# A hybrid decoder layer: both feed-forward products computed as 2x2 blocks with seven products each

## Chip, core and metric
One NeuronCore of one Trainium2 chip runs the whole program. The metric is the device time of one execution in microseconds (us). TensorE is called PE in the profile (PEld is its weight load), VectorE DVE, ScalarE ACT, GpSimd POOL, SyncE SP.

## What is computed
One step of a one-layer decoder trunk for two groups of requests: a prompt of 1024 tokens and 8 sampled sequences of 4 tokens. The kernel keeps them side by side as T = 1056 columns; activations lie transposed, channels on the 128 partitions. Two gated branches (windowed attention and a gated delta rule), then attention over a memory, then the part that is changed:

```
h = h + xo @ w_xo
u, gv = split(rmsnorm(h, norm_ffn_g) @ w_up, 2)        # w_up 1024 x 5632
u = causal_dwconv(u, ffn_conv_w)                       # 3 taps along the tokens
h = h + (silu(u) * gv) @ w_down                        # w_down 2816 x 1024
y = rmsnorm(h, final_norm_g)
```

With 128-wide tiles, w_up is 8 k tiles by 22 + 22 output tiles (FT = 22), and w_down is 22 k tiles by 8 output tiles.

## The kernel before
**Precision.** Each fp32 operand is split in two fp32r tiles, a head (the rounded value) and a rest (the value minus the head). A product is head x head + head x rest + rest x head, so each k tile of an output tile costs three matmuls for every chunk of columns. T is cut into NCH = 3 chunks of CW = 352 columns.

**Weights.** SP loads a slot of 128 x 1024 into RAW; GpSimd makes WH (head, L767/L768) and WL (rest, L771/L772) from it in pieces 256 wide (`split_pieces`; slots of the first stages in one instruction 1024 wide, L757/L759). Two slots alternate. A slot is free when PE has used it (`w_used`).

**Into the feed-forward.** `xo` is a product of 4 slots; each gives two output tiles, t = 0 to 7. VectorE adds each to H (L2565, `xo_free`), ScalarE makes its head times the gain (XH, L519) and its square (L456), VectorE the rest (XL, L524) and the sum of the squares (L464/L467). The first up product needs XH and XL of all eight. The norm's factor is applied after the product, so that the norm's sum (PE L480, ScalarE L488) is not in front of it.

**The loop.** A step f of 11 handles two tiles of u and two of gv. PE: four `gemm_tile` of 72 matmuls (L544), with PSUM banks 0 to 2 and 3 to 5 in turn, then `down(f-1)`: 8 output tiles, two k tiles each, 18 matmuls a tile (L1987). VectorE: per u tile the factor (L2591), the convolution over 1024 + 32 columns (L2598 to L2605), the product with gv out of PSUM (L2628), the rest of the activation (L2635); per output tile of `down` one addition of PSUM to H, 1056 wide (L2615, `fd_free`). ScalarE: three small copies of the convolution's edge, silu (L1279), the head of the activation (L1285). The last two k tiles of the down projection are computed by column chunks in `end_down` (L2019), each unit added to H (L2654), squared, summed and scaled for the final norm.

**Order.** Each engine runs its own list; semaphores alone bind them, and an engine that waits holds all that is behind it in its list.

## Time and profile before
| | |
|---|---|
| timed runs | 1998.45, 2003.45, 2004.74 us (median 2003.45) |
| profiled execution, first to last instruction | 2002.1 us |
| own time of the profiled execution outside that span | not listed; the median is 1.35 us above the span |
| busy: PE, PEld | 1891.3 us (94%), 1781.6 us (89%) |
| busy: VectorE, ScalarE, GpSimd | 958.1 us (48%), 489.9 us (24%), 832.1 us (42%) |
| feed-forward, from the last xo tile to the last down part | 1211.7 to 1961.3 us |

A busy share says how long an engine had an instruction in it. Matmuls overlap, so one is recorded for about twice the time between two starts; how fast PE goes is read from the distance of starts. In a group's row stand the count, the busy time and the mean ns of one, and behind the second bar the idle time of the engine just before them with what ended it. A wait is shown in square brackets in the timeline.

### The profile page before, as it was taken

How to read it: one execution, taken by the hardware profiler on the slowest of the kernel's cores; microseconds unless marked ns; L12 is line 12 of the kernel's file. 1: busy time of each engine (PE TensorE's matmuls, PEld its weight loads, DVE VectorE, ACT ScalarE, POOL GpSimd, SP SyncE). 2: the span in 40 equal slices, each digit the busy share in tenths (PEclk: the TensorE clock that was granted, in tenths of full speed). 3: DMA queues.
4: the chain of work that ended last, by engine and by line, in shares of the span. 5: the costliest groups of instructions: out<-in, count | busy, mean ns of one | idle time of the engine just before them, and what ended most of it. 6: DMA issues, size and time to landing. Idle time of an engine off the chain costs nothing.

```text
span 2002.1 us, 32389 instructions
## 1 busy us (share of the span) xinstructions
PE 1891.3 (94%) x13273; PEld 1781.6 (89%) x13273; DVE 958.1 (48%) x1150; ACT 489.9 (24%) x908; POOL 832.1 (42%) x907
## 2 busy tenths in 40 slices
PE   6988999999999899999998899999999999999997
PEld 5966799988878788998988599999999999999996
DVE  6877267754454132554142437443453444345346
ACT  6056326643232103421132423100100010000012
POOL 3411033421211233745753025654654565465455
PEclk9999999999999999999999999999999999999999
DMA  4311111110102131422223101111111111111112
GB/s 186 91 38 44 35 43 42 32 65 23 37 27 69 31 107 34 148 96 96 74 76 146 63 26 43 43 42 52 42 42 47 47 42 42 52 42 42 52 46 87
DMA packets 45483, 119.72 MB, mean 60 GB/s; under 512 B 3808, under 2 KB 20896, under 8 KB 44224
## 3 DMA queue, kind: packets, MB, share of 16 engines
q1 hardware_dynamic: 45392, 118.39, 17.7%
q8 instruction: 71, 1.16, 0.2%
q14 instruction: 20, 0.16, 0.0%
HBM read 102.94 MB, written 15.77 MB: 59 GB/s over the span
## 4 chain that ended last, share of the span: by engine, by line
PE 68%; DVE 7%; ACT 3%; issue 1%; POOL 0%; DVEq 0%; ACTq 0%; POOLq 0%
PE PS L544 42%; PE PS L1987 12%; PE PS L1378 3%; PE PS L1576 2%; PE PS L1870 1%; PE PS L1614 1%; PE PS L1770 1%; DVE XL L524 1%; ACT TMP L1223 1%; PE PS L1934 1%; DVE H L2650 1%; PE PS L1955 1%; PE PS L2019 1%; PE PS L1661 0%; PE PS L1927 0%
## 5 line engine op out<-in xcount | busy, mean ns | idle before, releaser
L767 POOL TENSOR_TENSOR WH<-RAW,CST 128x256 fp32r<-128x256 f32 x288 | 195.1, 705 | 827.4 <-PE PS L544 407.0
L544 PE MATMUL PS<-XH,WH 128*128 128x352 f32 x2280 | 505.3, 330 | 33.7 <-POOL WL L759 13.2
L544 PE MATMUL PS<-XH,WL 128*128 128x352 f32 x2280 | 493.0, 324 | 0.0
L544 PE MATMUL PS<-XL,WH 128*128 128x352 f32 x2280 | 492.4, 324 | 0.0
L544 PEld LDWEIGHTS PS<-XH,WH 128*128 128x128 f32 x2280 | 389.2, 190 | 51.7 <-issue 34.5
L544 PEld LDWEIGHTS PS<-XH,WL 128*128 128x128 f32 x2280 | 392.6, 188 | 0.0
L544 PEld LDWEIGHTS PS<-XL,WH 128*128 128x128 f32 x2280 | 388.7, 188 | 0.0
L771 POOL TENSOR_TENSOR WL<-RAW,WH 128x256 fp32r<-128x256 f32 x288 | 260.3, 931 | 7.5
L2615 DVE TENSOR_TENSOR H<-H,PS 128x1056 f32<-128x1056 f32 x80 | 100.3, 1254 | 130.5 <-PE PS L1987 130.5
L757 POOL TENSOR_TENSOR WH<-RAW,CST 128x1024 fp32r<-128x1024 f32 x22 | 45.2, 2055 | 265.2 <-PE PS L544 140.9
L1285 ACT ACTIVATE AH<-TMP 128x1056 fp32r<-128x1056 f32 x20 | 20.8, 1082 | 359.0 <-PE PS L1987 345.6
L1987 PE MATMUL PS<-AL,WH 128*128 128x352 f32 x480 | 104.2, 325 | 0.0
L1987 PE MATMUL PS<-AH,WL 128*128 128x352 f32 x480 | 103.6, 324 | 0.0
L1987 PE MATMUL PS<-AH,WH 128*128 128x352 f32 x480 | 103.4, 324 | 0.0
L2628 DVE TENSOR_TENSOR TMP<-TMP,PS 128x1056 f32<-128x1056 f32 x22 | 27.6, 1254 | 157.2 <-PE PS L544 157.1
L768 POOL TENSOR_TENSOR WH<-RAW,CST 128x256 fp32r<-128x256 f32 x96 | 90.4, 941 | 0.0
L1378 PE MATMUL PS<-XH,WH 128*128 128x352 f32 x240 | 86.5, 360 | 0.5
L2591 DVE TENSOR_TENSOR TMP<-PS,TMP 128x1056 f32<-128x1056 f32 x22 | 27.7, 1257 | 118.1 <-PE PS L544 118.1
L1987 PEld LDWEIGHTS PS<-AH,WH 128*128 128x128 f32 x480 | 82.0, 188 | 0.0
L1987 PEld LDWEIGHTS PS<-AL,WH 128*128 128x128 f32 x480 | 81.9, 188 | 0.0
L1987 PEld LDWEIGHTS PS<-AH,WL 128*128 128x128 f32 x480 | 81.7, 188 | 0.0
L1378 PE MATMUL PS<-XH,WL 128*128 128x352 f32 x240 | 77.6, 323 | 0.0
(464 smaller groups left out, 2683.8 us busy)
## 6 DMA issues: line engine op xcount, KB each, us to landing
RAW<-in_w SPq DMA_DIRECT2D x136, 512.0 KB, 3.5
H<-in_xT SPq DMA_DIRECT2D x4, 1056.0 KB, 9.1
TMP<-in_xT SPq DMA_DIRECT2D x2, 2112.0 KB, 8.5
early_gates<-DV SPq DMA_DIRECT2D x18, 176.0 KB, 1.9
out_yT<-H SPq DMA_DIRECT2D x4, 704.0 KB
early_gates<-A SPq DMA_DIRECT2D x12, 176.0 KB, 1.8
DV<-early_gates SPq DMA_DIRECT2D x1, 2112.0 KB, 14.2
TMP<-early_gates SPq DMA_DIRECT2D x2, 1056.0 KB, 5.4
```

The source lines that it names most:

```text
L544: mm = nc.tensor.matmul(PS[:, 3 * mm_g + c, 0:CW], w_[:, p, off + k * P:off + (k + 1) * P], x_[:, xk0 + k, c * CW:(c + 1) * CW], start=fir ...
L757: nc.gpsimd.tensor_tensor(WH[:, p, :], RAW[:, p, :], one, ALU.mult).then_inc(w_hi, 1)
L767: nc.gpsimd.tensor_tensor(WH[:, p, c], RAW[:, p, c], one[:, 0:PIECE], ALU.mult)
L768: nc.gpsimd.tensor_tensor(WH[:, p, cuts[-1]], RAW[:, p, cuts[-1]], one[:, 0:PIECE], ALU.mult).then_inc(w_hi, 1)
L771: nc.gpsimd.tensor_tensor(WL[:, p, c], RAW[:, p, c], WH[:, p, c].bitcast(F32), ALU.subtract)
L1285: nc.scalar.activation((LASTH if last else AH)[:, i, :], f_act[:, i, :], ACT.Copy).then_inc(f_hi, 1)
L1378: mm = nc.tensor.matmul(PS[:, GATE_BANKS[g >= GA], 0:CW], w_[:, p, k * P:(k + 1) * P], x_[:, k, c * CW:(c + 1) * CW], start=(k == 0 and w_ ...
L1576: mm = nc.tensor.matmul(PS[out, bank + i, HP * j:HP * j + HP], lhs(h, r), rhs(h, r), start=True, stop=True)
L1987: mm = nc.tensor.matmul(PS[:, 3 * (m % 2) + c, 0:CW], w_[:, p, (m % 4) * 256 + k * P:(m % 4) * 256 + k * P + P], x_[:, k, bass.ts(c, CW)], ...
L2591: nc.vector.tensor_tensor(wide(x[:, 2:2 + T]), acc(i), wide(f_rs), ALU.mult).then_inc(fu_free, 1)
L2615: nc.vector.tensor_tensor(wide(H[:, m, :]), wide(H[:, m, :]), acc(m % 2), ALU.add).then_inc(fd_free, 1)
L2628: nc.vector.tensor_tensor(wide(f_act[:, i, :]), wide(f_act[:, i, :]), acc(i), ALU.mult).then_inc(f_gate, 1)
```

## The change
Let A be weights and B activations, each cut in 2x2 blocks: for the up product A's rows are k tiles 0-3 and 4-7 and its columns the pair (u tile t, gv tile t); B's columns are the token halves of HT = 528. With S1 = A21 + A22, S2 = S1 - A11, S3 = A11 - A21, S4 = A12 - S2 and the like T1 to T4 of the activations, seven block products give all four output blocks. One such set is called a pair here: 22 pairs for the up product, then 12 pairs (2 output tiles each) for the down projection, in three groups (`DOWN`) of 4, 3 and 3 k tiles a half.

- **PE.** `product` runs kh k tiles x 3 x 2 matmuls of QT = 264 columns for one block product (kh = 4 or 3). Products 0, 2, 4, 6 of a pair accumulate in the same two banks, and are read in between; 1 and 3 share two banks, 5 has its own.
- **ScalarE** makes the heads of the seven weight blocks (128 x 512, `head`, into a ring of 5 places), reads products 0, 1 and 2 of an up pair out of PSUM (`up_read`), and does edge copies and silu (`mlp_u`, `mlp_silu`) of the pair before.
- **GpSimd** makes the seven rests only (`block_rest`).
- **VectorE** makes the four weight sums of the next pair (`block_sums`, 128 x 512), adds products 3, 4, 5 (`up_read`), then does `mlp_conv` (the factor now from SBUF to SBUF) and `mlp_gate`: two halves of 528, and one or three differences of halves, T1 to T4 of the activations.
- **SP** loads four blocks of 256 KB a pair (`block_loads`), and stores the seven activation blocks of each two tiles to DRAM (`spills`); half of H is stored too, as its place is used, and loaded again in the down part. For each down group they are loaded as `units` of 128 x 528 (28, 21 and 21 of them, and 4 for the last two k tiles), from 5 and later 9 places; ScalarE makes the head of each and VectorE the rest, up to three behind one product (`unit_rests`). The places 0 to 4 are the space of the even tile's buffers.
- **VectorE in the down part** adds each of the seven products of a pair to a half tile of H (`down_read`, 528 wide).
- **In front**, xo's tiles come in the order 0, 4, 1, 5, ...; for each pair of tiles five blocks with head and rest are made, and two more behind the loop (`xb[6]`, `xb[5]`). The weight heads of the first up pair stand behind that loop in ScalarE's list.
- `end_down` keeps its form, with weights from the ring.

Core of the diff ("up_act" and "heads_after" on ScalarE are as told above):

```diff
+PRODUCTS = ("A11 B11", "S1 T1", "S2 T2", "S4 B22", "S3 T3", "A12 B21", "A22 T4")
+NP7 = len(PRODUCTS)
+HT = T // 2
+QT = T // 4
+BLK = 4 * P
+UPAIRS = FT
+DOWN = ((4, 0), (3, 8), (3, 14))
+DPAIRS = 4 * len(DOWN)
+NPAIRS = UPAIRS + DPAIRS
+LAST_BLOCKS = 4
...
+            return {0: 6 * p, 2: 6 * p, 4: 6 * p, 6: 6 * p, 1: 2, 3: 2, 5: 4}[i]
...
+                pool.wait_ge(q_hi, m + 1)
+                hi, lo = ring[ring_slot(p * NP7 + i if src is None else m)]
+                src = block_source(i, p % 2) if src is None else src
+                nc.gpsimd.tensor_tensor(lo[:, 0:w], src[:, 0:w], hi[:, 0:w].bitcast(F32), ALU.subtract).then_inc(q_lo, 1)
...
+                act.wait_ge(xo_free, t + 1)
+                if t % 2 == 0:
+                    wait(act, fx_lo, 5 * j)
+                    wait(act, fx_t, 4 * j)
+                    nc.scalar.activation(x_g, H[:, k, :], ACT.Copy, scale=g).then_inc(fx_g, 1)
+                    in_head(xb[0][:, j, :], H[:, k, 0:HT], g)
+                else:
+                    in_head(xb[3][:, j, :], H[:, k, HT:T], g)
+                if t >= 2:
+                    act.wait_ge(nadd, 21 + max(1, t - 2))
+                nc.scalar.activation(f_sq[t % 2], H[:, k, :], ACT.Square).then_inc(nsq, 1)
+                if t % 2 == 0:
+                    act.wait_ge(fx_t, 4 * j + 1)
+                    in_head(xb[1][:, j, :], x_t1)
+                else:
+                    act.wait_ge(fx_t, 4 * j + 2)
+                    in_head(xb[2][:, j, :], x_t2)
+                    act.wait_ge(fx_t, 4 * j + 3)
+                    in_head(xb[4][:, j, :], x_g[:, 0:HT])
...
+            head(0, 0, 0, 0)
+            head(1, 1, 0, 0)
+            head(2, 2, 0, 0)
+            act.wait_ge(fx_t, 16)
...
+            def product(m, i, p, kh, at_, ready=None):
+                pe.wait_ge(q_lo, m + 1)
+                hi, lo = x_block(i, kh)
+                wh, wl = ring[ring_slot(at_)]
+                for k in range(kh):
+                    if ready is not None:
+                        pe.wait_ge(fx_lo, ready(k))
+                    for w_, x_ in ((wh, hi), (wh, lo), (wl, hi)):
+                        for c in range(2):
+                            first = k == 0 and w_ is wh and x_ is hi
+                            last = k == kh - 1 and w_ is wl
+                            mm = nc.tensor.matmul(PS[:, bank(i, p) + c, 0:QT], w_[:, k * P:(k + 1) * P],
+                                                  x_[:, k, c * QT:(c + 1) * QT], start=first and i in (0, 1, 5), stop=last,
+                                                  skip_group_check=True)
+                mm.then_inc(q_mm, 1)
...
+                    if i == 0:
+                        if isinstance(n, int) and n < 2:
+                            pe.wait_ge(xo_free, 7) if n == 0 else pe.wait_ge(nln, 4)
+                        else:
+                            pe.wait_ge(f_gate, 2 * (n - 2) + 1)
+                    elif i == 1:
+                        pe.wait_ge(xo_free, 8) if first else pe.wait_ge(u_rv, 3 * (n - 1) + 1)
+                    elif i == 5:
+                        pe.wait_ge(nln, 4) if first else pe.wait_ge(u_rv, 3 * n)
+                    elif i == 6:
+                        pe.wait_ge(u_rv, 3 * n + 2)
                     else:
-                        pe.wait_ge(fu_free, 2 * f + j - 1)
-                    if first and j == 1:
-                        pe.wait_ge(nln, 4)
-                    if first and j == 0:
-                        pe.wait_ge(xo_free, 7)
-                    gemm_tile(j % 2, j % 2, 0, KT, 0, ready=(nlo, 24) if first and j == 0 else None, turn=TURN,
-                              between=(lambda: norm_sum(pe, 3), KT - 2) if first and j == 0 else None).then_inc(w_used, 1)
-                if not first:
-                    down(f - 1, FFN0(f) + 4)
-            mlp_pe(0)
-            with pe.Fori(1, FT // 2) as f:
-                mlp_pe(f)
-            end_down(NSLOTS - 2)
+                        pe.wait_ge(u_ra, 3 * n + i - 1)
...
+                if part == 0:
+                    dve.wait_ge(q_raw["a11"], Q_RAW["a11"] + 16 * (n + 1))
+                    dve.wait_ge(q_raw["a21"], Q_RAW["a21"] + 16 * (n + 1))
+                    if first:
+                        dve.wait_ge(w_used, NSLOTS - 1)
+                    else:
+                        dve.wait_ge(q_lo, base + 5)
+                    out(nc.vector.tensor_tensor(sum_3[:, w], raw_a11[:, w], raw_a21[:, w], ALU.subtract))
+                    dve.wait_ge(q_raw["a22"], Q_RAW["a22"] + 16 * (n + 1))
+                    out(nc.vector.tensor_tensor(raw_a21[:, w], raw_a21[:, w], raw_a22(p)[:, w], ALU.add))
+                if part == 1:
+                    dve.wait_ge(q_sum, 4 * n + 2)
+                    if not first:
+                        dve.wait_ge(q_lo, base + 7)
+                    out(nc.vector.tensor_tensor(sum_2(p)[:, w], raw_a21[:, w], raw_a11[:, w], ALU.subtract))
+                if part == 2 or part == 1 and not first:
+                    dve.wait_ge(q_raw["a12"], Q_RAW["a12"] + 16 * (n + 1))
+                    dve.wait_ge(q_sum, 4 * n + 3)
+                    if first:
+                        dve.wait_ge(nadd, 28)
+                    out(nc.vector.tensor_tensor(s4_buf[:, w], raw_a12[:, w], sum_2(p)[:, w], ALU.subtract))
...
+                nc.vector.tensor_tensor(wide(H[:, k, :]), wide(H[:, k, :]), acc(t % 2), ALU.add).then_inc(xo_free, 1)
+                if t % 2 == 0:
+                    dve.wait_ge(fx_g, j + 1)
+                    nc.vector.tensor_tensor(x_t1, x_g[:, HT:T], x_g[:, 0:HT], ALU.subtract).then_inc(fx_t, 1)
+                    dve.wait_ge(fx_hi, 5 * j + 1)
+                    in_rest(xb[0][1][:, j, :], H[:, k, 0:HT], xb[0][0][:, j, :], g)
+                    if t >= 2:
+                        ffn_add(t - 1)
+                    dve.wait_ge(fx_hi, 5 * j + 2)
+                    in_rest(xb[1][1][:, j, :], x_t1, xb[1][0][:, j, :])
+                    if t == 6:
+                        block_sums(0, 0, 0)
+                        block_sums(0, 0, 1)
+                else:
+                    dve.wait_ge(xo_free, t + 1)
+                    dve.wait_ge(fx_t, 4 * j + 1)
+                    nc.vector.scalar_tensor_tensor(x_t2, H[:, k, HT:T], g, x_t1, ALU.mult, ALU.subtract).then_inc(fx_t, 1)
+                    nc.vector.scalar_tensor_tensor(x_g[:, 0:HT], H[:, k, HT:T], g, x_g[:, HT:T], ALU.mult, ALU.subtract).then_inc(fx_t, 1)
+                    dve.wait_ge(fx_t, 4 * j + 2)
+                    nc.vector.scalar_tensor_tensor(x_t4[j], H[:, k, 0:HT], g, x_t2, ALU.mult, ALU.subtract).then_inc(fx_t, 1)
+                    dve.wait_ge(fx_hi, 5 * j + 3)
+                    in_rest(xb[3][1][:, j, :], H[:, k, HT:T], xb[3][0][:, j, :], g)
+                    dve.wait_ge(fx_hi, 5 * j + 4)
+                    in_rest(xb[2][1][:, j, :], x_t2, xb[2][0][:, j, :])
+                    if t >= 2:
+                        ffn_add(t - 1)
+                    if t == 7:
+                        ffn_add(7)
+                        block_sums(0, 0, 2)
+                    dve.wait_ge(fx_hi, 5 * j + 5)
+                    in_rest(xb[4][1][:, j, :], x_g[:, 0:HT], xb[4][0][:, j, :])
...
+            def up_dve(n, p, half):
+                last = isinstance(n, int) and n == UPAIRS - 1
+                block_sums(n + 1, 1 - p, 0)
+                up_read(n, 3, p)
+                block_sums(n + 1, 1 - p, 1)
+                up_read(n, 4, p)
                 if last:
-                    rests()
-                if not (isinstance(f, int) and f == 0):
-                    mlp_down(f - 1, FFN0(f) + 4)
-                if not last:
-                    rests()
-            mlp_dve(0)
-            with dve.Fori(1, FT // 2 - 1) as f:
-                mlp_dve(f)
-            mlp_dve(FT // 2 - 1)
+                    for i in range(4):
+                        unit_rests(NP7 * n + i)
+                up_read(n, 5, p)
+                if last:
+                    unit_rests(NP7 * n + 4)
+                    unit_rests(NP7 * n + 5)
+                mlp_conv(n, p)
+                if isinstance(n, int) and n < 2:
+                    scale_h(2 * n)
+                    scale_h(2 * n + 1)
+                mlp_gate(n, p, half)
...
+            for n in range(UPAIRS, NPAIRS):
+                for i in range(NP7):
+                    down_read(n, i)
+                    if n + 1 < NPAIRS and i in (0, 3):
+                        block_sums(n + 1, (n + 1) % 2, i // 3)
+                    unit_rests(NP7 * n + i)
+                    if n == UPAIRS + 1 and i in (3, 4, 5, 6):
+                        scale_h(i + 1)
```

## Rows read from the trace of the kernel before
**Rows 1.** The page: span, and busy time, share of the span and instructions of each engine.
```profile
span 2002.1 us, 32389 instructions
...
PE 1891.3 (94%) x13273; PEld 1781.6 (89%) x13273; DVE 958.1 (48%) x1150; ACT 489.9 (24%) x908; POOL 832.1 (42%) x907
```

**Rows 2.** Windows: us, then busy us (and instructions) of each engine, granted clock, DMA share.
```profile
1226.00:1961.00 735.00, 735.00 (x4541) 734.87 (x4540) 322.88 (x309) 63.16 (x117) 400.69 (x504) 1.00 0.14 45
```

**Rows 3.** Groups of matmuls by form, 1211.7 to 1962 us (count | busy us, mean ns).
```profile
L544 PE MATMUL PS<-XH,WH 128*128 128x352 f32 x1056 | 228.7, 325 | 0.0
...
L1987 PE MATMUL PS<-AL,WH 128*128 128x352 f32 x480 | 104.2, 325 | 0.0
...
L480 PE MATMUL PS<-TMP,CST 128*128 128x352 f32 x6 | 2.0, 476 | 1.3 <-DVE TMP L467 1.3
```

**Rows 4.** Timeline of PE, memory keys and values: start us, us, instruction.
```profile
920.90 0.40 PE L1870 MATMUL PS<-WH,AH 128*128 128x512 f32 x1
...
923.47 0.39 PE L1870 MATMUL PS<-WL,AH 128*128 128x512 f32 x1
```

**Rows 5.** Timeline of PE, narrower fp32 matmuls; last row: ns min/median/max of one line.
```profile
1109.19 2.05 PE L1919 MATMUL PS<-TMP,DV 128*128 128x128 f32 x16 [0.74 <-ACT TMP L1231]
1111.08 1.89 PE L1902 MATMUL PS<-DV,TMP 128*128 128x256 f32 x8
...
L1902 PE MATMUL PS<-DV,TMP x64: 379/379/483, 1081.8 to 1123.7; 128*128 128x256 f32 x64
```

**Rows 6.** Groups of VectorE by form, 1211.7 to 1962 us.
```profile
L2603 DVE SCALAR_TENSOR_TENSOR TMP<-TMP,CST 128x1024 f32<-128x1024 f32 x44 | 68.2, 1551 | 0.0
L2605 DVE SCALAR_TENSOR_TENSOR TMP<-TMP,CST 128x32 f32<-128x32 f32 x44 | 30.4, 690 | 0.0
L2635 DVE TENSOR_TENSOR AL<-TMP,AH 128x1056 fp32r<-128x1056 f32 x20 | 28.4, 1457 | 0.0
L2591 DVE TENSOR_TENSOR TMP<-PS,TMP 128x1056 f32<-128x1056 f32 x22 | 27.7, 1257 | 118.1 <-PE PS L544 118.1
```

**Rows 7.** One line's instructions: GpSimd's rests, 256 and 1024 wide (ns min/median/max).
```profile
L759 POOL TENSOR_TENSOR WL<-RAW,WH x22: 2344/2728/3290, 9.8 to 370.2; 128x1024 fp32r<-128x1024 f32 x22
...
L771 POOL TENSOR_TENSOR WL<-RAW,WH x195: 727/738/1754, 1215.4 to 1965.4; 128x256 fp32r<-128x256 f32 x195
```

**Rows 8.** Timeline of VectorE and of GpSimd where both work, 1213 to 1234 us.
```profile
1213.11 5.07 DVE L524 SCALAR_TENSOR_TENSOR XL<-H,CST,XH 128x1056 fp32r<-128x1056 f32 x3
...
1233.63 0.24 DVE L2605 SCALAR_TENSOR_TENSOR TMP<-TMP,CST 128x32 f32<-128x32 f32 x1
...
1215.42 5.05 POOL L771 TENSOR_TENSOR WL<-RAW,WH 128x256 fp32r<-128x256 f32 x3
```

**Rows 9.** Groups of ScalarE by form, 1170 to 1962 us.
```profile
L1285 ACT ACTIVATE AH<-TMP 128x1056 fp32r<-128x1056 f32 x20 | 20.8, 1082 | 359.0 <-PE PS L1987 345.6 <-DVE TMP L2628 13.4
...
L456 ACT ACTIVATE TMP<-H 128x1056 f32<-128x1056 f32 x8 | 8.6, 1080 | 13.1 <-DVE H L2565 13.1
```

**Rows 10.** Timeline of VectorE: the last two additions of the xo product.
```profile
1206.07 1.25 DVE L2565 TENSOR_TENSOR H<-H,PS 128x1056 f32<-128x1056 f32 x1 [3.40 <-PE PS L544]
...
1211.89 1.25 DVE L2565 TENSOR_TENSOR H<-H,PS 128x1056 f32<-128x1056 f32 x1 [3.40 <-PE PS L544]
```

**Rows 11.** Windows and timeline of PE around one idle stretch of 2.5 us.
```profile
1144.00:1148.00 4.00, 1.91 (x7) 1.94 (x8) 3.97 (x2) 0.00 (x0) 0.00 (x0) 0.77 0.92 375
1148.00:1152.00 4.00, 4.00 (x22) 4.00 (x21) 1.77 (x4) 2.10 (x2) 0.00 (x0) 0.80 0.03 12
...
1146.09 0.53 PE L1934 MATMUL PS<-XH,WH 128*128 128x352 f32 x1 [2.54 <-DVE TMP L2543]
```

**Rows 12.** Timeline where the last down projection begins.
```profile
1963.37 0.52 DVE L2654 TENSOR_TENSOR H<-H,PS 128x352 f32<-128x352 f32 x1 [0.23 <-PE PS L2019]
...
1966.83 0.58 PE L2019 MATMUL PS<-YAR,WH 128*128 128x352 f32 x2 [1.59 <-POOL WL L772]
```

**Rows 13.** DMA issues: KB each, median us from issue to landing.
```profile
RAW<-in_w SPq DMA_DIRECT2D x136, 512.0 KB, 3.5
```

More of the change, by code:

```diff
@@ L366, in build @@
+        u_g2 = [TMP[:, 2626:2626 + HT], h_flat[:, 2114:2114 + HT]]
+        t_a, t_b = h_flat[:, 2642:2642 + HT], h_flat[:, 3170:3170 + HT]
+        assert 2626 + HT <= R_AT and R_AT + 4 * BLK <= 5 * T
+        x_g = TMP[:, R_AT:R_AT + T]
+        x_t1, x_t2 = [TMP[:, R_AT + T + HT * i:R_AT + T + HT * i + HT] for i in range(2)]
+        x_t4 = [TMP[:, 6 * T + HT * j:6 * T + HT * j + HT] for j in range(4)]
         take = carve(5 * T)
         f_hist = take(FT * NB * 2, "p (t b n) -> p t b n", t=FT, b=NB)
-        f_one = take(1)
@@ L741, in _ @@
+            for b in range(LAST_BLOCKS):
+                last_load(b)
             for c in range(NCH):
@@ new lines, in _ @@
+            up_act(0, 0)
+            up_act(1, 1)
+            with act.Fori(1, FT // 2 - 1) as j:
+                up_act(2 * j, 0)
+                up_act(2 * j + 1, 1)
+            up_act(FT - 2, 0)
+            up_act(FT - 1, 1)
+            for n in range(UPAIRS, NPAIRS):
+                if n == UPAIRS:
+                    mlp_u(UPAIRS - 1, 1)
+                    unit_heads(NP7 * UPAIRS - 1)
+                for i in range(NP7):
+                    heads_after(n, i, n % 2)
+                    unit_heads(NP7 * n + i)
+                    if n == UPAIRS and i == 0:
+                        mlp_silu(UPAIRS - 1, 1)
@@ L2002, in end_sum, with end_down @@
                 for u in direct:
[L2003 to L2004 removed]
+                    pe.wait_ge(e_sqr, E_SQR + u + 1)
+                    mm = nc.tensor.matmul(PS[:, 6 + c % 2, 0:CW], ones, e_sq[u % 6], start=False, stop=u == direct[-1])
                 mm.then_inc(e_sum, 1)
[L2007 to L2009 removed]
+            def end_down():
@@ L2052, in _ @@
+            up_pe(0, 0)
+            up_pe(1, 1)
+            with pe.Fori(1, FT // 2) as j:
+                up_pe(2 * j, 0)
+                up_pe(2 * j + 1, 1)
+            for n in range(UPAIRS, NPAIRS):
+                down_pe(n)
+            end_down()
         @block.vector
@@ L2561, in _ @@
+            g_ffn = cst("g_ffn")
+            xb = [x_block(i, 4) for i in range(NP7)]
+            for t, k in enumerate(XO_ORDER):
+                j = t // 2
+                g = g_ffn[:, k:k + 1]
                 if t % 2 == 0:
```

718 lines of the change are left out of this document (554 added, 164 removed).

## The prediction
> **What bounds the kernel now.** I read the page's busy line first, for which engine fills the span [rows 1]: PE does, 94%. Then the windows: for 735 us of the feed-forward PE has 4541 recorded matmuls and no idle time [rows 2], so they start 735 / 4541 = 0.1619 us apart. VectorE is busy 323 us there, GpSimd 401, ScalarE 63: cover, not path. The groups by form give the counts: 3 x 1056 matmuls in the up product and 3 x 480 in the down loop, 4608 in all [rows 3]. 4608 x 0.1619 = 746.0 us; the norm's sum adds 2.0 and a wait of 1.3 [rows 3]: 749.3, against 749.6 from the end of xo to `end_down` (1211.7 to 1961.3). So the feed-forward is matmul starts and nothing else; whatever shortens them counts in full, and whatever makes PE wait counts in full too.
>
> **The matmuls.** After: 22 x 7 x 4 x 6 = 3696 for up and (4 x 4 + 4 x 3 + 4 x 3) x 7 x 6 = 1680 for down, 5376 of 264 columns. No fp32r matmul of 264 stands in the trace. From 352 to 512 columns the distance grows from 0.1619 to (923.47 - 920.90) / 11 = 0.2336 us [rows 4], 0.448 ns a column; carried down, 264 columns take 0.1619 - 88 x 0.000448 = 0.1225 us. A weight load of 128 columns per matmul stays: sixteen 128-wide records fill the 1.89 us to the next group's start, 0.118 us each with one load each [rows 5], so the load is hidden at 0.1225, by 4 ns only. I take 0.1225: same type, same operands as the two rows it is drawn from. 5376 x 0.1225 = 658.6 us; bounds 598 and 673.
>
> The Trainium skill (TensorE: Matmul & The Clock Gate, section "Back-to-back issue gap") gives N / 2.4 + 2.5 ns for a matmul by itself: an estimate of 112.5 ns here and 604.8 us for the sum. By that rule 352 columns would take 149.2 ns; the trace has 161.9, so it disagrees.
>
> **In front, before the first product.** The last xo tile ends 0.2 us before the addition at 1211.89 [rows 10], and before the change PE goes straight on. Additions come 5.82 us apart with VectorE idle 3.40 of it [rows 10]. After, VectorE's list per two tiles is two additions, four differences, five rests of 528 and two square sums. A 1056-wide one takes 1.25 [rows 6, 10], less about 0.05 of overlap; a 528-wide one by the 352 row (0.52) and this about 0.70, in a string 0.61. With the waits for ScalarE's x_g and heads (1.08 for 1056 [rows 9], 0.64 for 528) that is 5.4 for the even tile and 6.0 for the odd one, 11.4 of 11.65 available; GpSimd's last two slots of xo cost some 5 more in all (contention, below). So VectorE comes late by about 5.5 us at t = 6, which then carries three weight sums (1.9) ahead of the addition of t = 7. I put that addition at 7 us behind the tile's end. Behind it ScalarE does head, square, two heads (3.0), then the first weight head (0.6), GpSimd its rest (1.3), and only then PE can start: 7 + 1.2 + 4.9 = 13 us. GpSimd's other rests, the two blocks behind the loop and the norm's chain run behind products 0 to 4. Bounds: VectorE on time, 6; twice as late, 20. Take 13.
>
> **Per up pair.** PE needs 7 x 24 x 0.1225 = 20.6 us. GpSimd: a 512-wide rest, between 0.727 for 256 and 2.344 for 1024 [rows 7], 1.27; seven are 8.9. ScalarE: seven heads, three reads of 0.64, silu 1.08, edges: under 9 (352 to 1056 wide at 1.08 [rows 9]). VectorE alone: four sums 2.4, three reads 2.1, convolution 5.0 (the factor 1.2, three taps of 1.0 to 1.2, three of 32 columns at 0.24), gate 1.3, differences 1.2 on average: 12.0. What is added is contention. VectorE's three two-input operations of 1056 took 5.07 us and GpSimd's three rests 5.05 [rows 8] in the same stretch, where alone they take 3.6 and 2.1: they take turns. An operation of 32 columns takes 0.24 when free [rows 8] and 0.690 on average [rows 6]; with an operand in PSUM (L2591) the average is 1.257, as alone, against 1.457 from SBUF [rows 6]. If every rest of GpSimd holds VectorE up for its whole length, 12.0 + 8.9 = 20.9 us a pair: just above PE's 20.6. So VectorE cannot pace the loop by much, but its order can: product 6 waits for the read of product 4, which stands behind the reading of product 3 and two sums, and these behind gate and differences of the pair before. With contention I follow that list to 36.9 us after the pair before began, against 38.1 when PE asks: 1.2 us to spare in the odd pair, about 3 in the even. Blocks of 256 KB land in well under a product and a half (512 KB in 3.5 us [rows 13]) and are asked for over a product ahead. I charge 6 us of small waits over the 22 pairs; bounds 0 and 35 (the list late by about 1.6 us in every pair, since one GpSimd rest in the wrong place costs up to 1.27).
>
> **Up to down.** VectorE's list between product 4 of the last up pair and the first read of the down part: one read, 10 units of 0.61, a read, 5 units, convolution (8 with contention, by the means in [rows 6]), silu on ScalarE 1.1, gate 1.4, 2 units, first `down_read` 0.7: 22.8 us, plus 1.5 us as units 5 to 9 are loaded only when the rests of 0 to 4 have freed their places, and 2 us of contention: 26.3. PE has four products of its own to run in that time, 11.8 us. It stands 14.5 us before product 2 of the first down pair, and about 1.5 more before product 3, behind 3 units and two sums: 16. Bounds 5 (units early) and 25.
>
> **The clock.** After 2.54 us of idle PE the granted clock is 0.77 and 0.80 in the two windows of 4 us about and behind it [rows 11], PE at its lower level of 1.2 GHz for a part of each: 4 x 0.23 + 4 x 0.20 = 1.7 us lost. Two long waits: 3.4 us.
>
> **Down.** At kh = 3 a product is 18 x 0.1225 = 2.2 us. VectorE beside it: a read 0.7, sums 0.3; with two units a product 1.2 more, 2.2, and GpSimd's rest (1.0) takes turns with it. That lasts 4 products of the second group and 11 of the third: I charge 0.4 to 0.5 each, 7 us; bounds 1 and 15. The four `scale_h` in the second down pair: 1.5.
>
> **Last part.** `end_down` is the same; PE's wait of 1.59 us for a GpSimd split before [rows 12] (PE starts at 1966.83, WL late) should go, as the ring's last blocks are ready early: -1.6.
>
> **Sum.** After: 658.6 + 2.0 (norm sum) + 13 + 6 + 16 + 3.4 + 7 + 1.5 = 707.5 us, against 749.6: -42.1, and -1.6: -43.7. The profiled span of 2002.1 gives 1958.4; the median of the runs stands 1.35 above that span, so 1960 us.
>
> **Rivals.**
> 1. *The waits are hidden.* If VectorE keeps pace in front and at the turn to down (bounds 6, 5, 0, 1): 1960 - 7 - 11 - 6 - 6 = 1930. For: ScalarE is almost idle. Against: the lists above are longer than PE's work beside them. Chance 0.12, for 1925 to 1940.
> 2. *Narrow matmuls cheaper.* 0.1113 for 264 columns takes 60 us more: 1900. For: the fp32 rows. Against: the fp32r rows at both widths, 9 to 10% above 2.4 GHz. 0.05.
> 3. *VectorE sets the pace of the up pairs.* A late read in every pair, 1 to 1.7 us: 22 to 37 us more than charged, less the 6: 1976 to 1992. For: 1.2 us to spare only. 0.17.
> 4. *Slower than before.* The same place, the read of product 4 behind two sums that wait for the fourth block's load and a rest. PE stands once a pair; from 6 + 44 us, 2.3 us a pair, the gain is gone; at 3 us a pair the time is 1960 - 6 + 66 = 2020. Against: 20.9 is all VectorE can need, unless loads come late. 0.07.
> 5. *No change to be told*: the chain of 3 at its upper end, 0.03.
> My forecast, 1940 to 1976: 0.56.
>
> A difference under 0.3% (6 us) is about what a measurement of this kernel cannot tell from none. Faster: 0.56 + 0.12 + 0.05 + 0.17 = 0.90; same 0.03; slower 0.07. The range leaves out half of rival 1's lower end, rival 2 and rival 4: 1930 to 1992.
>
> **What would show it.** Starts of the 264-wide matmuls 0.1225 us apart, 5376 of them; a PE gap of 6 to 20 us before the first, released by GpSimd behind a ScalarE head; a gap of 5 to 25 in the first down pair released by VectorE; clock below 1 behind both; in the loop waits of PE for VectorE near product 6 under 0.3 us a pair; GpSimd's rest near 1.3 to 2. I am wrong if the distance is off by more than 3 ns (16 us), or if the loop has a wait in every product.

## The result, and the profile after

The changed kernel takes 1992.92 us (median of 5 runs, 1990.78 to 1997.97), the kernel before on the same chip 2003.51. The ratio is 0.9951, 95% interval 0.9931 to 0.997: faster, by 10.6 us where 43.5 were forecast, and 0.9 us outside the range of 1930 to 1992. The page of the changed kernel, to read beside [rows 1]:

```profile
span 1990.9 us, 35520 instructions
...
PE 1817.4 (91%) x14041; PEld 1699.2 (85%) x14041; DVE 1206.2 (61%) x1506; ACT 694.0 (35%) x1292; POOL 748.6 (38%) x621
```

PE's busy time falls by 74 us, the span by 11: PE now waits. Where it waits is seen by the distance of matmul starts. Here is the timeline of PE at the first product of pairs 23 and 25, and where the last part begins:

```profile
1749.45 1.26 PE L2462 MATMUL PS<-XH,WL 128*128 128x264 f32 x9
...
1790.42 1.26 PE L2462 MATMUL PS<-XH,WH 128*128 128x264 f32 x9
...
1951.93 0.32 PE L2443 MATMUL PS<-XH,RING 128*128 128x352 f32 x1
```

Between the first two lie two pairs of 168 matmuls without a wait: 40.97 / 336 = 0.1219 us each, and the undisturbed products stand at 0.1217. All 5376 are 654.1 us. What a product takes more than 0.1217 us a matmul, counted from its own first start to that of the next product, is called its loss here; a wait ahead of product 6 is thus loss of product 5. From the first product (1227.12) to `end_down` (1951.9) there are 724.8 us: 70.7 are loss.

| us | forecast | measured |
|---|---|---|
| idle in front of product 0 | 13 | 13.4 |
| 5376 matmuls | 658.6 | 654.1 |
| loss in pair 0 (norm sum 2.0, clock 1.7) | 3.7 | 11.8 |
| loss in up pairs 1 to 21 | 6 | 16.2 |
| loss in pair 22, the first down pair (waits 16, clock 1.7) | 17.7 | 24.2 |
| loss in pairs 23 to 33 (7 and 1.5) | 8.5 | 18.5 |
| sum | 707.5 | 738.2 |
| xo itself, two waits of 0.9 us for VectorE | 0 | +1.9 |
| last part | -1.6 | -1.8 |

Before, the same stretch took 749.6: -11.4, plus 1.9, less 1.8, is -11.3, and the spans differ by 11.2. The places of loss follow in order of time. In front, to read beside [rows 10]: VectorE, ScalarE, GpSimd, then PE.

```profile
1212.50 1.25 DVE L3081 TENSOR_TENSOR H<-H,PS 128x1056 f32<-128x1056 f32 x1
...
1220.02 1.25 DVE L3081 TENSOR_TENSOR H<-H,PS 128x1056 f32<-128x1056 f32 x1
...
1223.98 0.62 ACT L1603 ACTIVATE WL<-RAW 128x512 fp32r<-128x512 f32 x1
...
1224.74 2.29 POOL L1088 TENSOR_TENSOR WL<-RAW,WL 128x512 fp32r<-128x512 f32 x1 [29.18 <-ACT WL L1603]
...
1227.12 5.03 PE L2462 MATMUL PS<-XH,WL 128*128 128x264 f32 x24 [13.39 <-issue]
```

The last tile of xo ends at 1213.7, its addition starts 6.3 us behind that, the weight head 4.0 later, GpSimd's rest takes 2.3: the chain as forecast. In pair 0, product 6, with VectorE's wait behind it:

```profile
1254.81 4.71 PE L2462 MATMUL PS<-XL,WH 128*128 128x264 f32 x24 [2.71 <-DVE TMP L3129]
...
1248.94 1.72 DVE L3058 TENSOR_TENSOR SUMS<-RAW 128x512 f32<-128x512 f32 x1 [9.33 <-DMA RAW<-in_wf]
```

VectorE stands 9.3 us for the blocks of pair 1, and the read of product 4 is behind that. SP's list shows why: the 2 MB store of H's upper half goes out immediately ahead of them.

```profile
1239.64 0.38 SPq L934 DMA_DIRECT2D h_spill<-H  x1
1240.12 0.45 SPq L898 DMA_DIRECT2D RAW<-in_wf  x1
```

In the up loop every second pair, the even one, waits ahead of product 6. Here is VectorE's list from the gate of the tile before to the read of product 4 (L3129), with one rest of GpSimd and then PE:

```profile
1415.90 0.70 DVE L3173 TENSOR_TENSOR H<-H,PS 128x528 f32<-128x528 f32 x1 [1.15 <-ACT H L1688]
1416.52 0.70 DVE L3174 TENSOR_TENSOR H<-H 128x528 f32<-128x528 f32 x1
1417.26 1.68 DVE L3183 TENSOR_TENSOR TMP<-H,TMP 128x528 f32<-128x528 f32 x1
1418.87 1.79 DVE L3185 TENSOR_TENSOR H<-H 128x528 f32<-128x528 f32 x1
...
1424.02 1.67 DVE L3071 TENSOR_TENSOR TMP<-RAW 128x512 f32<-128x512 f32 x1
1425.60 0.69 DVE L3129 TENSOR_TENSOR TMP<-TMP,PS 128x528 f32<-128x528 f32 x1
...
1418.34 1.75 POOL L1088 TENSOR_TENSOR WL<-RAW,WL 128x512 fp32r<-128x512 f32 x1
...
1426.43 1.35 PE L2462 MATMUL PS<-XL,WH 128*128 128x264 f32 x9 [0.89 <-DVE TMP L3129]
```

VectorE is never idle for more than 0.15 us from the gate to the read. Three operations of 0.7 us take 1.7 to 1.8 here. Each begins while GpSimd has a rest under way and ends 0.6 us behind the end of that rest (GpSimd's ends at 1420.09, VectorE's at 1420.66): VectorE waits the rest out, as in the turns of [rows 8]. The loss is 1.6 us in each even pair and 0.02 in the odd ones.

At the turn from up to down come PE, then ScalarE and VectorE ahead of the first down read (L3254), then PE's clock (windows: us, busy us and count of PE, PEld, DVE, ACT, POOL, clock, DMA share, GB/s), to read beside [rows 11]:

```profile
1709.35 3.19 PE L2462 MATMUL PS<-XL,WH 128*128 128x264 f32 x24 [1.41 <-POOL WH L1088]
1730.51 5.65 PE L2462 MATMUL PS<-YAR,WL 128*128 128x264 f32 x24 [17.98 <-DVE H L3254]
...
1714.34 0.64 ACT L1648 ACTIVATE DVR<-TMP 128x528 fp32r<-128x528 f32 x1 [4.91 <-DMA TMP<-acts]
...
1715.01 0.71 DVE L3206 TENSOR_TENSOR DVR<-TMP,DVR 128x528 fp32r<-128x528 f32 x1 [3.53 <-ACT DVR L1648]
...
1729.77 0.69 DVE L3254 TENSOR_TENSOR H<-H,PS 128x528 f32<-128x528 f32 x1
...
1704.83:1749.45 44.62, 23.93 (x171) 23.36 (x169) 34.67 (x43) 19.41 (x35) 14.57 (x10) 0.77 0.58 200
...
1716.00:1736.00 20.00, 5.49 (x25) 5.49 (x26) 17.30 (x22) 7.84 (x16) 6.68 (x4) 0.50 0.44 148
```

In the 20 us from 1716, 14.5 of them idle, the granted clock is 0.50, the level of 1.2 GHz, and product 2 behind the wait begins at that level: it takes 5.65 us where the one before took 3.19, and loses 2.5. In the down groups, at the change from the first to the second, and what PE waited for from 1755 to 1925 us in all:

```profile
1818.80 3.79 PE L2462 MATMUL PS<-YAR,WL 128*128 128x264 f32 x18 [2.51 <-DVE H L3254]
...
PE PS L2462 <- DVE H L3254: 13.7, 12, 2.5
```

In the kernel before, PE had no idle time from 1226 to 1961 [rows 2].

### The profile page after: what moved, and what is told of

Read it like the earlier page. It is cut to its first block and busy times, and to the rows that moved or that the text cites. A ratio compares the mean times of both kernels' runs of the same rounds, so it can differ in the third digit from the quotient of the medians.

```text
span 1990.9 us, 35520 instructions
## 1 busy us (share of the span) xinstructions
PE 1817.4 (91%) x14041; PEld 1699.2 (85%) x14041; DVE 1206.2 (61%) x1506; ACT 694.0 (35%) x1292; POOL 748.6 (38%) x621
## 5 line engine op out<-in xcount | busy, mean ns | idle before, releaser
L696 PE MATMUL PS<-XH,WH 128*128 128x352 f32 x1224 | 275.5, 333 | 37.8 <-POOL WL L1040 14.0
L696 PE MATMUL PS<-XH,WL 128*128 128x352 f32 x1224 | 264.6, 324 | 0.0
L696 PE MATMUL PS<-XL,WH 128*128 128x352 f32 x1224 | 264.1, 324 | 0.0
L696 PEld LDWEIGHTS PS<-XH,WH 128*128 128x128 f32 x1224 | 208.0, 190 | 56.0 <-issue 35.6
L1048 POOL TENSOR_TENSOR WH<-RAW,CST 128x256 fp32r<-128x256 f32 x90 | 65.7, 757 | 483.2 <-PE PS L1818 196.1
L696 PEld LDWEIGHTS PS<-XL,WH 128*128 128x128 f32 x1224 | 208.6, 189 | 0.0
L2462 PE MATMUL PS<-XH,WL 128*128 128x264 f32 x1296 | 169.4, 287 | 13.4 <-issue 13.4
L1088 POOL TENSOR_TENSOR WL<-RAW,WL 128x512 fp32r<-128x512 f32 (+1 forms) x66 | 104.9, 1589 | 137.1 <-ACT WL L1603 135.4
L2462 PEld LDWEIGHTS PS<-XL,WH 128*128 128x128 f32 x648 | 82.4, 192 | 17.3 <-issue 11.3
L3254 DVE TENSOR_TENSOR H<-H,PS 128x528 f32<-128x528 f32 x84 | 58.5, 699 | 62.4 <-PE PS L2462 62.4
L2462 PE MATMUL PS<-XL,RING 128*128 128x264 f32 x720 | 93.0, 284 | 0.6 <-DVE H L3254 0.6
L1818 PE MATMUL PS<-XH,WH 128*128 128x352 f32 x240 | 87.2, 363 | 0.5
L1818 PE MATMUL PS<-XH,WL 128*128 128x352 f32 x240 | 78.1, 325 | 0.0
L1818 PE MATMUL PS<-XL,WH 128*128 128x352 f32 x240 | 78.0, 325 | 0.0
L1052 POOL TENSOR_TENSOR WL<-RAW,WH 128x256 fp32r<-128x256 f32 x90 | 76.9, 882 | 2.4
```

The source lines that it names most:

```text
L696: mm = nc.tensor.matmul(PS[:, 3 * mm_g + c, 0:CW], w_[:, p, off + k * P:off + (k + 1) * P], x_[:, xk0 + k, c * CW:(c + 1) * CW], start=fir ...
L1048: nc.gpsimd.tensor_tensor(WH[:, p, c], RAW[:, p, c], one[:, 0:PIECE], ALU.mult)
L1052: nc.gpsimd.tensor_tensor(WL[:, p, c], RAW[:, p, c], WH[:, p, c].bitcast(F32), ALU.subtract)
L1088: nc.gpsimd.tensor_tensor(lo[:, 0:w], src[:, 0:w], hi[:, 0:w].bitcast(F32), ALU.subtract).then_inc(q_lo, 1)
L1818: mm = nc.tensor.matmul(PS[:, GATE_BANKS[g >= GA], 0:CW], w_[:, p, k * P:(k + 1) * P], x_[:, k, c * CW:(c + 1) * CW], start=(k == 0 and w_ ...
L2462: mm = nc.tensor.matmul(PS[:, bank(i, p) + c, 0:QT], w_[:, k * P:(k + 1) * P], x_[:, k, c * QT:(c + 1) * QT], start=first and i in (0, 1, ...
```

## The experiments

All start from the changed kernel and, unless told, only move instructions. A kernel's verdict rests on the losses of its one trace: where xo ends, ahead of all that was edited, moves by up to 9 us between executions (1210.8 to 1219.9), so spans tell little. The ratios are to the kernel before, run beside each kernel, so ratios compare better than times. Time, ratio with its interval, and losses by place (front is the idle time ahead of product 0, the other columns are pairs):

| | us | ratio | front | pair 0 | 1-21 | 22 | 23-33 |
|---|---|---|---|---|---|---|---|
| changed kernel | 1992.92 | 0.9951 (0.9931-0.997) | 13.4 | 11.8 | 16.2 | 24.2 | 18.5 |
| e1 heads ahead | 1997.21 | 0.9956 (0.9936-0.9976) | 5.6 | 20.2 | 16.2 | 25.4 | 16.4 |
| e2 PE kept busy | 1993.08 | 0.9945 (0.9925-0.9964) | 13.4 | 11.9 | 16.3 | 27.9 | 14.2 |
| e3 sum behind read | 1978.39 | 0.9865 (0.9838-0.9892) | 13.4 | 8.7 | 4.4 | 26.2 | 17.9 |
| e4 turn, first order | 1988.58 | 0.9912 (0.9883-0.9941) | 13.4 | 11.7 | 16.2 | 24.5 | 16.8 |
| e5 loads before store | 1992.27 | 0.9928 (0.9905-0.9951) | 13.4 | 7.4 | 16.2 | 25.3 | 17.5 |
| e6 e5 and e1 | 1989.15 | 0.9934 (0.9917-0.995) | 5.6 | 14.2 | 16.1 | 27.2 | 16.1 |
| e7 turn, second order | 1993.16 | 0.9944 (0.9924-0.9964) | 13.4 | 11.7 | 16.2 | 22.8 | 16.9 |
| e8 blocks further ahead | 1988.16 | 0.9923 (0.9907-0.994) | 13.4 | 11.6 | 16.2 | 25.7 | 7.1 |
| e9 e3, e5, e7, e8 | 1966.62 | 0.9802 (0.978-0.9824) | 13.4 | 7.2 | 4.5 | 20.6 | 7.0 |
| e10 e7, thin rests | 1982.28 | one run | 13.3 | 11.7 | 16.3 | 15.8 | 15.1 |
| e11 e9, GpSimd helps | 1967.65 | 0.9808 (0.9786-0.983) | 13.3 | 7.4 | 4.6 | 25.1 | 6.7 |
| e12 thin differences | 1983.15 | 0.9889 (0.9857-0.992) | 13.4 | 11.8 | 5.8 | 25.3 | 17.4 |

Where nothing is edited, pair 0 loses 11.6 to 11.8 and pairs 1 to 21 16.1 to 16.3 in every trace; pair 22 loses 24.2 to 27.9 and the down pairs behind it 14.2 to 18.5, so there a difference under some 4 us between two traces says nothing.

**e1: the idle in front of product 0.**
```diff
@@ ScalarE, xo loop, t == KT - 1
+                if t == KT - 1:
+                    head(0, 0, 0, 0)
                 act.wait_ge(xo_free, t + 1)
+                if t == KT - 1:
+                    head(1, 1, 0, 0)
```

> The first weight heads of the first up pair are moved ahead in ScalarE's list: head 0 before the last xo tile's work, head 1 at its start. Theory (the chain that stands in ScalarE's list holds PE): the 13.4 us idle before the first product shrinks to about 3, product 1 starts when VectorE has added the last xo tile and GpSimd has the rest of block 1, product 2 behind the norm's sum, about 7 us earlier than now: 6 to 9 us off the time, the clock's part included. Rival (VectorE is late by itself, and what it still has to make sets product 5): product 0 starts early and PE waits later in the same pair instead, 0 to 2 us off.

Product 0 came 7.8 us nearer to xo's end, and pair 0 lost 8.4 us more, as the rival had it. The forecast's chain, with the weight head behind ScalarE's list, was right, but it was not what set the start of pair 1.

**e2: the clock in front.** 55 matmuls of fp32 with constants go to a PSUM bank that is free.
```diff
+WARM = 55
...
+                        if first:
+                            for _ in range(WARM):
+                                nc.tensor.matmul(PS[:, 7, 0:P], ones, ident, start=True, stop=True)
```

> 55 matmuls of 128 x 128 fp32 on constants into a free bank fill PE's idle time before the first product; nothing else changes. Theory (the slow first product is PE's clock, half after the idle stretch): product 0 takes 2.9 us and not 4.9, and if the two later half-clock stretches of the first pair go too, 2 to 5 us off. Rival (products of the first pair are slow because their operands or weights come late): product 0 stays at 4.9 us, no change in the time.

Windows about product 0 in the changed kernel, then in e2, where product 0 starts at 1224.18 (the clock is the third number from the end):

```profile
1218.00:1232.00 14.00, 4.88 (x25) 4.91 (x26) 13.69 (x15) 6.47 (x11) 6.23 (x3) 0.53 0.00 1
```

```profile
1226.00:1246.00 20.00, 17.61 (x136) 16.76 (x135) 10.88 (x10) 12.70 (x17) 7.77 (x7) 1.00 0.42 151
```

Product 0 lost 0.07 us where it had lost 1.94, product 4 lost 0.1 where it had lost 1.6, and product 5 lost 5.7 instead of 2.9: pair 0 as before. With the clock high or low, product 6 starts 41.1 us behind xo's end. The Trainium skill (TensorE: Matmul & The Clock Gate, section "What's actually happening") has PE at 1.2 GHz after it has idled. The changed kernel's windows agree (0.53 above, 0.50 at the turn), and so does e2, where PE was kept busy and the clock stays at 1.00 (from 1224 to 1230 too). But the time that the higher clock gave back to product 0 was lost again before product 6.

**e5 and e6: that event.**
```diff
+            block_loads(1, 1, 0)
             sp.wait_ge(fx_lo, 28)
             sp.dma_start(d["h_spill"].rearrange("k p t -> p k t"), H[:, 4:8, :]).then_inc(h_out, 16)
-            block_loads(1, 1, 0)
             block_loads(1, 1, 1)
```

> One edit in SP's list: the loads of pair 1's first three blocks are issued before the 2 MB store of H's upper half instead of behind it. Theory (pair 1 starts late because VectorE waits 9.3 us for these loads, which stand behind the store in SP's list and in the DMA queues): VectorE's idle <-DMA RAW<-in_wf before the first sums of pair 1 falls below 3 us, the stretch from the last addition of the attention's output to pair 1's first product falls from 45.8 to 40 to 43 us, and the kernel is 3 to 6 us faster than the changed one, about 1987 to 1990. Rival (the late heads and rests of pair 0 set its end, and the loads arrive while nothing needs them): the idle of VectorE goes but the stretch stays within 1 us of 45.8 and the time within the noise of 1993.

> The same order of SP, and in addition the first two weight heads of pair 0 moved ahead in ScalarE's list, as in e1_front_heads, where the 7.8 us that product 0 started earlier were lost again before pair 1. Theory (they were lost to the late loads of pair 1): now the front gains both, the stretch from the last addition to pair 1 falls to 35 to 40 us and the time to 1983 to 1988. Rival (what took the 7.8 us was pair 0's own chain: GpSimd's rests, the norm and the reads): the stretch stays at 43 us or more, no better than e5_spill_order.

SP and VectorE in e5:

```profile
1232.99 0.33 SPq L898 DMA_DIRECT2D RAW<-in_wf  x1
...
1245.59 0.38 SPq L935 DMA_DIRECT2D h_spill<-H  x1
...
1245.48 0.68 DVE L3058 TENSOR_TENSOR SUMS<-RAW 128x512 f32<-128x512 f32 x1
```

The blocks are there when VectorE comes, the losses of products 5 and 6 (2.9 and 1.6 us) are gone, and from xo's end to pair 1 it is 41.2 us instead of 45.6. The first load goes out 13.3 us behind xo's end instead of 26.4, and no longer behind 2 MB; how much of the 4.4 us was SP's wait for what the store needs, and how much the store's own transfer, was not told apart. The timed median moved by 0.7 us only (4.6 by the ratios), inside its spread, and the intervals of the two ratios overlap: the gain is read from the trace alone. With the heads ahead too (e6) the stretch is 40.3 us, near the upper end of the theory's 35 to 40 and not at the rival's 43: of the 7.8 us only 0.9 is kept. The reason that the rival gave holds for the rest: in e6 PE waits 3.0 us for the norm's square sums and 3.5 for ScalarE's read, pair 0's own chain. Whether e2's matmuls pay beside e5, where the late blocks are gone, was not run.

**e3 and e12: the up loop.** e3 moves the fourth weight sum behind the read of product 4.
```diff
-                if part == 2 or part == 1 and not first:
+                if part == 2:
...
                 up_read(n, 4, p)
+                block_sums(n + 1, 1 - p, 2)
```

> In VectorE's list the fourth weight sum of the next pair goes behind the read of product 4, in front of which it stood (the down pairs keep their order). Theory (PE's 1.1 us before product 6 of each even pair is the place of that sum in the list): the wait of 1.1 us and the smaller ones behind it go in ten even pairs, 9 to 16 us off. Rival (VectorE and GpSimd together have no time left in the pair, 20.9 us of work at the worst): the wait comes back at another product of the pair, 0 to 3 us off.

e12 keeps the order and leaves out most of the four activation differences: 32 of 528 columns are computed.
```diff
-                    nc.vector.tensor_tensor(t_b, y[:, HT:T], t_a, ALU.subtract).then_inc(f_t, 1)
+                    nc.vector.tensor_tensor(t_b[:, 0:32], y[:, HT:HT + 32], t_a[:, 0:32], ALU.subtract).then_inc(f_t, 1)
```

> The changed kernel with the four activation differences of each two up pairs only 32 of 528 columns wide: part of these subtractions is left out, all orders and waits stay. They take VectorE some 0.6 us each, 2.4 a period, three of them ahead of the even pair's reads 3 and 4. Theory (the 1.6 us that each even pair loses before product 6 is VectorE's list being that much too long ahead of the read of product 4, and e3's order was worth what the work itself is): the even pairs' loss falls from 1.6 to below 0.5 us, the up pairs' loss from 28.0 to 12 to 14, and the time by 13 to 16 us, as in e3_loop_order. Rival (what holds the read of product 4 is the sums and the loads for them, not the differences): the loss stays above 1 us in each even pair and the time within 4 us of 1993.

VectorE in e3, at the place of the list above:

```profile
1416.68 0.69 DVE L3065 TENSOR_TENSOR RAW<-RAW 128x512 f32<-128x512 f32 x1
1417.28 0.70 DVE L3129 TENSOR_TENSOR TMP<-TMP,PS 128x528 f32<-128x528 f32 x1
1417.89 1.18 DVE L3071 TENSOR_TENSOR TMP<-RAW 128x512 f32<-128x512 f32 x1
```

The loss falls from 16.2 to 4.4 us in pairs 1 to 21, and to 5.8 in e12: both take the same wait away, and PE's list of waits over these pairs is empty in both. The order alone was enough: one operation behind the read instead of in front of it. e3's interval lies wholly below the changed kernel's; the median is 14.5 us lower (17 by the ratios), and the trace saves 11.8 here and 3.1 in pair 0, whose product 6 stood behind the same sum.

e12 fell short of its own numbers: pairs 0 to 21 lose 17.6 us in all where 12 to 14 were expected, and the median is 9.8 us lower (12 by the ratios), not 13 to 16. Its VectorE, at the same two differences, shows one reason:

```profile
1414.20 1.17 DVE L3183 TENSOR_TENSOR TMP<-H,TMP 128x32 f32<-128x32 f32 x1
1415.29 1.32 DVE L3185 TENSOR_TENSOR H<-H 128x32 f32<-128x32 f32 x1
```

With a sixteenth of the columns they still take 1.2 and 1.3 us, where 1.7 and 1.8 stood: beside a rest of GpSimd most of such an operation's time is the wait for that rest, and the third one, with no rest beside it, falls from 0.7 to 0.2.

**e4, e7, e10, e11: the turn.** e4 puts reads 0 and 1 of the first down pair ahead of the last convolution.
```diff
@@ VectorE, last up pair
                     unit_rests(NP7 * n + 5)
+                    down_read(n + 1, 0)
+                    unit_rests(NP7 * n + 6)
+                    down_read(n + 1, 1)
+                    unit_rests(NP7 * n + 7)
                 mlp_conv(n, p)
```

> At the turn from up to down VectorE reads products 0 and 1 of the first down pair, and makes the rests of the units behind them, before the convolution and gate of the last up pair; ScalarE's heads of these units and SP's loads of them are moved ahead accordingly. Theory (PE's 18 us before product 2 of the first down pair is the length of VectorE's list in front of the first read): product 2 starts 12 to 15 us earlier, PE then waits 5 to 8 us before product 5 for the units whose places the convolution frees, 7 to 11 us off the time. Rival (the total of VectorE's work at the turn is what counts, wherever it stands): the whole wait returns before product 4 or 5, under 3 us off.

```profile
1742.32 0.81 PE L2463 MATMUL PS<-AH,RING 128*128 128x264 f32 x2 [17.62 <-DVE H L3225]
...
1733.44 0.33 SPq L1006 DMA_DIRECT2D act_last<-H  x1
1733.81 0.43 SPq L752 DMA_DIRECT2D out_ffn_tail<-TMP  x1
1736.85 3.65 SPq L980 DMA_DIRECT2D TMP<-acts  x8
```

The wait went from product 2 to product 4, as long as before: the read of product 2 stood behind the rests of blocks which SP loads only behind the last activation's store, that is, behind convolution and gate. e7 mends that too.
```diff
@@ SP
+            sp.wait_ge(fp_ok, 3 * FT)
+            store(d["ffn_tail"], f_tail)
+            units_due(NP7 * FT + 2)
             sp.wait_ge(f_gate, 2 * FT)
             sp.dma_start(d["act_last"][1], u_act[1]).then_inc(sp_o, 16)
-            sp.wait_ge(fp_ok, 3 * FT)
-            store(d["ffn_tail"], f_tail)
@@ VectorE, last up pair
                 mlp_conv(n, p)
...
+                if last:
+                    down_read(n + 1, 2)
                 mlp_gate(n, p, half)
```

> The turn from the up to the down projection in another order than e4_turn: VectorE reads products 0 and 1 of the first down pair and takes the rests of all activation blocks that lie in the first five places ahead of the last convolution, and product 2's read ahead of the last gate; SP stores the tail and loads the blocks of the next places before it stores the last activation; ScalarE's list to match. Theory (e4's 17.9 us came from loads that stood behind the last activation's store in SP's list): the first down pair's loss falls from 24.2 to 6 to 14 us, the time to 1982 to 1988. Rival (VectorE's own work in the turn, some 30 us of convolution, gate, sums, rests and reads, is the bound whatever its order): the loss stays above 20 us and the time within the noise of 1993.

e10 keeps that order and leaves out part of the rests: 32 of 528 columns of each are computed (its edit has HT = 528; the 264 in its expectation is a slip). e11 gives 8 of the 28 rests to GpSimd.
```diff
+                    w = slice(0, 32 if u < 28 else HT)
+                    nc.vector.tensor_tensor(lo[:, w], unit_place[PLACES[u]][:, w], hi[:, w].bitcast(F32), ALU.subtract).then_inc(un_lo, 1)
@@ e11, GpSimd, behind a block rest of its own
+                    if m in POOL_AFTER:
+                        pool.wait_ge(un_hi, POOL_AFTER[m] + 1)
+                        unit_rest(nc.gpsimd, POOL_AFTER[m]).then_inc(un_lp, 1)
```

> e7's order, with the rests of the 28 activation blocks of the first down group only 32 of 264 columns wide: part of that subtraction is left out, everything else stays. It takes some 0.45 us each, 12 in all, from VectorE around the turn. Theory (VectorE's own work, 86% and more of the turn's time, sets the first down pair's pace, whatever its order): the pair's loss falls from 22.8 to 8 to 13 us. Rival (late loads and ScalarE's heads set it): the loss stays above 18 us and VectorE idles instead.

> e9, with 8 of the 28 rests of the first down group given to GpSimd, one behind a block rest of its own. A rest takes VectorE 0.7 us and GpSimd 1.3 to 1.6. Theory (VectorE's own work is the bound of the turn and GpSimd has time there): the first down pair's loss falls by 3 to 6 us against e9, and the time by as much. Rival (GpSimd's rests come late, or slow VectorE as much as they relieve it): the loss stays within 1 us of e9's or grows.

Windows over the first down pair in e7, then e10:

```profile
1710.76:1754.00 43.24, 28.67 (x171) 27.49 (x170) 33.77 (x43) 19.93 (x35) 14.82 (x10) 0.80 0.70 234
```

```profile
1706.24:1742.49 36.25, 23.48 (x170) 22.31 (x169) 22.30 (x42) 19.68 (x35) 13.33 (x10) 0.91 0.68 219
```

e7 breaks the one wait of 18 us into smaller losses, 1.6 to 5.3 us at each of the seven products, and the sum is 22.8: only 1.4 less, which is inside what unedited kernels differ by. So the rival's figure came, and two other orders of the lists, e4's and e7's, won nothing. VectorE is busy 78% of that stretch. In e10, of which there is one run and one trace, VectorE is busy 11.5 us less and the loss falls by 7.0, between what the two theories gave: VectorE's own work is a part, and it waits 11 us of the 36 for ScalarE's heads of blocks. e11 lost 25.1 against e9's 20.6, and its time is the same within 1 us: the rival was right that nothing is won. One part of that shows: GpSimd's block rest for product 1 stood behind a rest that waited for its head, and PE waited 4.0 us for it where it waited 2.7 in e9.

```profile
1692.99 1.12 POOL L580 TENSOR_TENSOR YAR<-TMP,YAR 128x528 fp32r<-128x528 f32 x1 [10.20 <-ACT YAR L1669]
1694.07 1.77 POOL L1106 TENSOR_TENSOR WH<-RAW,WH 128x512 fp32r<-128x512 f32 x1
...
1695.98 4.62 PE L2487 MATMUL PS<-XL,WH 128*128 128x264 f32 x24 [3.96 <-POOL WH L1106]
```

**e8: the changes of down group.** SP waits at a weight load for a place to come free, and the activation blocks behind it wait along.
```diff
-                units_due(NP7 * n + 4)
+                units_due(NP7 * n + 6)
                 if n + 2 < NPAIRS:
                     block_loads(n + 2, n % 2, 0)
...
-                units_due(NP7 * n + 7)
+                units_due(NP7 * n + 8)
```

> In SP's list for the down pairs, the loads of activation blocks go two to three products further ahead of the weight loads that wait for a rest (units through slot 6 instead of 4, then through slot 8 instead of 7). Theory (at the two changes of group, 5.9, 4.6 and 5.1 us are lost to reads that stand on VectorE behind rests whose blocks arrive late): the losses of pairs 25 to 31 fall from 18.3 to below 10 us, the time by 5 to 9 us to 1984 to 1988. Rival (VectorE's and ScalarE's own work at a change of group is too long for the product, loads in time or not): the losses stay above 14 us and the time within 2 us of 1993. The first down pair's block loads also move a little, so its 24 us may change by 2 either way.

SP's issues at the first change of group, changed kernel, then e8; then PE's waits in e8 from 1760 to 1925:

```profile
1808.32 0.33 SPq L907 DMA_DIRECT2D SUMS<-in_wf  x1
1808.69 2.80 SPq L980 DMA_DIRECT2D TMP<-acts  x6
```

```profile
1803.32 0.33 SPq L911 DMA_DIRECT2D RAW<-in_wf  x1
1803.69 5.72 SPq L980 DMA_DIRECT2D TMP<-acts  x10
...
PE PS L2462 <- DVE H L3254: 4.5, 6, 1.2
```

The blocks come ahead of the weights: about the change of group ScalarE waits 1.6 us for them, where it waited 9.5. The loss falls from 18.5 to 7.1, far outside the 14.2 to 18.5 of all kernels without the edit.

**e9: the orders together.**

> Four orders together: the sum for product 6's block behind the read (e3), pair 1's loads ahead of the store of H's upper half (e5), the turn's second order (e7) and the loads of activation blocks further ahead (e8). If their places don't touch, the losses over bare matmuls add up: from 70.7 us in the changed kernel, less 15 (e3), 4 (e5), 1.4 (e7) and 11 (e8) to 37 to 42, and the time to 1960 to 1970. If one gives back what another wins (VectorE's work pushed into the next place), the losses stay above 50 and the time above 1972.

The losses add up as expected: 39.3 us in all, against 70.7. 1966.62 us is 2.0% under the kernel before, and the interval lies wholly below the changed kernel's. Only pair 22's 20.6 is still large.

## Why the prediction was wrong

- **What bounds the kernel before** and that every wait of PE would count in full: right. The balance of starts and losses closes to 0.1 us.
- **Matmuls, 0.1225.** 0.1217 measured, 4.5 us less in all. Carrying the distance down from 352 and 512 columns held. The Trainium skill's rule for a matmul by itself (TensorE: Matmul & The Clock Gate, section "Back-to-back issue gap"), by which 112.5 ns was the estimate, is 9 ns short of this trace. Rivals 1, 2, 4 and 5 are out.
- **Front, 13 us:** 13.4, by the chain that was told. Two of its parts were off and cancelled: the addition came 6.3 us behind the tile's end, not 7, and GpSimd's rest took 2.3, not 1.3.
- **Up pairs, "1.2 us to spare in the odd pair, about 3 in the even": the step that failed in the loop.** The places are the other way round: the even pair has the wait, the odd one has none. My sum has the differences at their mean, 1.2 us a pair, but three of the four stand in front of the even pair's reads. Contention fell on two of these and on the fourth sum, 1.7 to 1.8 us each, and the read held product 6 up by 1.1 us. The up pairs lose 16.2 us instead of 6, within my bound of 35. Rival 3 ends at 1992, 0.9 us from the measured time, but that is chance: no pair was paced by VectorE, every second one met one read behind one operation too many, and the loop has only a third of the miss.
- **Pair 0: a term that was missing.** I charged norm and clock, 3.7 us, and no load; 4.4 us of the 11.8 were pair 1's blocks behind a store in SP's list (e5). I had asked whether blocks of 256 KB land in time, not what SP issues ahead of them. The 7.4 left in e5 are 2.1 and 1.6 on products 0 and 4, the two that e2 made fast with the clock at 1.00, 1.5 for the norm's sum, 1.9 ahead of product 4 for ScalarE's read, and 0.3.
- **Turn, 16:** the mechanism was right (read 0 behind units, convolution and gate), the size was 18.2 + 1.6 + 1.5 = 21.3 of waits with the clock's 2.5 on top, against 1.7. The long wait was 18.0 where I had 14.5. The short one that I put before product 3 did not come; two others did, 1.4 before product 1 for GpSimd and 1.3 before product 6. The term for late blocks, 1.5 us, was too low: ScalarE stood 4.9 us for one load and VectorE 3.5 behind it.
- **Down groups, "I charge 0.4 to 0.5 each, 7 us": the other step that failed.** That term and the 1.5 for `scale_h` make 8.5; measured were 18.5, above my bound of 15 for the first. The 11.4 us that e8 took away were loads, held in SP's list behind weight loads that waited for a place, a wait that my list of VectorE's work had no term for. The 7.1 us left in e8 are about what I charged; that they are VectorE's own work was not shown.
- **Last part, -1.6:** -1.8.

Of the 32.5 us missing in the span, 10.2 are the loop, 10.0 the down groups, 8.1 pair 0 and 6.5 the turn, 2.3 are xo's and the front's; 4.5 came back by the matmuls. What holds pair 22 at 20 us is open in part: e10 shows that VectorE's rests are some 7 of it, and whether the rest is ScalarE's heads, their loads or the clock was not told apart.
